# Turning queries and keys on VectorE in 32x32 blocks in place of TensorE

## What is computed

```python
xn = rms_norm(x, norm_mix[l])
proj = xn @ w_in[l]
qa, ka, va, oa, if_pre, qb, kb, vb, gates = jnp.split(proj, IN_SPLITS, axis=-1)
h_a = mlstm_chunkwise(heads(qa, 4), heads(ka, 4), heads(va, 4), ig, lf)   # 4 heads, dqk 128
qh = rms_norm(heads(qb, 8), norm_q_moba[l])                               # 8 heads, dh 128
kh = rms_norm(heads(kb, 8), norm_k_moba[l])
h_b = moba_attention(qh, kh, heads(vb, 8))
...
merged = g[..., :D] * (h_a @ w_branch_a[l]) + g[..., D:] * (h_b @ w_branch_b[l])
x = x + merged @ w_out[l]
x = x + jnp.square(jax.nn.relu(rms_norm(x, norm_mlp[l]) @ w_up[l])) @ w_down[l]
```

## Time and profile before

| | |
|---|---|
| Median of 3 runs | 1382.12 us (1382.01 to 1382.16) |
| Profiled execution | 1381.83 us, its span 1380.0 us |
| TensorE busy | 1374.2 us, 100% of the span |
| VectorE busy | 740.3 us, 54% |
| ScalarE busy | 624.2 us, 45% |
| Granted TensorE clock | full in every slice of the span |
| HBM | 187 GB/s over the span |

### The profile page before, as it was taken

The page is one execution under the profiler, slowest core; times in us unless marked ns, Lnnn a source line. Parts: engine busy times, 40 slices in busy tenths (PEclk is TensorE's granted clock), DMA queues, the critical chain, the costliest instruction groups (busy, mean ns, idle before and its releaser), DMA issues.

```text
span 1380.0 us, 17281 instructions
## 1 busy us (share of the span) xinstructions
PE 1374.2 (100%) x6655; PEld 1154.1 (84%) x6655; DVE 740.3 (54%) x741; ACT 624.2 (45%) x713; POOL 20.5 (1%) x35
## 2 busy tenths in 40 slices
PE   9999999999999999999999999999999999999999
PEld 7888888888888888888888888888888888888887
DVE  5566555544655454555565656544445656544443
ACT  5545455464444444445444444333334444443332
POOL 1111000000000000000000000000000000000000
PEclk9999999999999999999999999999999999999999
DMA  8555554545655555555555555555565555565562
GB/s 277 188 190 184 181 174 158 178 156 179 244 183 192 196 191 182 195 182 195 179 192 186 182 183 183 196 199 184 198 197 183 183 182 186 185 205 185 190 205 92
DMA packets 132549, 258.73 MB, mean 187 GB/s; under 512 B 6250, under 2 KB 8340, under 8 KB 132244
## 3 DMA queue, kind: packets, MB, share of 16 engines
q1 hardware_dynamic: 130336, 257.97, 56.5%
q10 hardware_dynamic: 2164, 0.09, 0.1%
HBM read 255.94 MB, written 2.10 MB: 187 GB/s over the span
## 4 chain that ended last, share of the span: by engine, by line
PE 99%; DMA 0%; DVE 0%; ACT 0%; issue 0%; SPq 0%; ACTq 0%
PE ps L871 23%; PE ps L873 23%; PE ps L872 23%; PE ps L894 17%; PE ps L889 9%; PE ps L903 2%; DMA rows<-in_x_dram 0%; PE ps L923 0%; PE ps L971 0%; PE ps L1028 0%; PE ps L991 0%; PE ps L990 0%; PE ps L989 0%; PE ps L970 0%; PE ps L1017 0%; PE ps L1016 0%
## 5 line engine op out<-in xcount | busy, mean ns | idle before, releaser
L603 DVE TENSOR_TENSOR w_lo<-raw,w_hi 128x1024 fp32r<-128x1024 f32 x480 | 587.6, 1225 | 601.6 <-ACT w_hi L364 600.4
L364 ACT ACTIVATE w_hi<-raw 128x1024 fp32r<-128x1024 f32 x480 | 508.9, 1061 | 722.2 <-PE ps L873 524.4
L894 PE MATMUL ps<-xT,w_hi 128*128 128x512 f32 x1024 | 360.5, 398 | 0.0
L889 PE MATMUL ps<-xT,w_lo 128*128 128x256 f32 x1024 | 284.9, 281 | 0.0
L871 PE MATMUL ps<-w_hi,xT 128*128 128x512 f32 x640 | 254.9, 398 | 0.7 <-DVE w_lo L603 0.7
L873 PE MATMUL ps<-w_hi,xT 128*128 128x512 f32 x640 | 249.7, 390 | 0.0
L872 PE MATMUL ps<-w_lo,xT 128*128 128x512 f32 x640 | 249.2, 389 | 0.0
L894 PEld LDWEIGHTS ps<-xT,w_hi 128*128 128x128 f32 x1024 | 191.4, 188 | 46.1
L889 PEld LDWEIGHTS ps<-xT,w_lo 128*128 128x128 f32 x1024 | 193.4, 189 | 1.5
L871 PE MATMUL ps<-w_hi,merged 128*128 128x512 f32 x384 | 149.7, 390 | 0.0
L871 PE MATMUL ps<-w_hi,branch 128*128 128x512 f32 x384 | 149.5, 389 | 0.0
(11 more groups left out here) (173 smaller groups left out, 586.2 us busy)
## 6 DMA issues: line engine op xcount, KB each, us to landing
raw<-in_w_in_dram SPq DMA_DIRECT2D x79, 1024.0 KB, 5.1
raw<-in_w_up_dram SPq DMA_DIRECT2D x64, 1024.0 KB, 5.4
raw<-in_w_down_dram SPq DMA_DIRECT2D x64, 1024.0 KB, 5.0
raw<-in_w_out_dram SPq DMA_DIRECT2D x16, 1024.0 KB, 5.0
raw<-in_w_branch_b_dram SPq DMA_DIRECT2D x8, 1024.0 KB, 5.0
raw<-in_w_branch_a_dram SPq DMA_DIRECT2D x8, 1024.0 KB, 5.0
rows<-in_x_dram SPq DMA_DIRECT2D x8, 256.0 KB, 7.9
rows<-in_x_dram SPq DMA_DIRECT2D x1, 2048.0 KB, 8.0
```

What stands on the lines that cost most here:

```text
L364: act.activation(w_hi[:, k % RING, :, :], raw[:, k // 2, KH * (k % 2):KH * (k % 2) + KH, :], ACT.Copy).then_inc(hi_made, 1)
L603: dve.tensor_tensor(w_lo[:, k % RING, :, :], raw[:, k // 2, KH * (k % 2):KH * (k % 2) + KH, :], w_hi[:, k % RING, :, :].bitcast(F32), ALU. ...
L889: return pe.matmul(ps[:, q0 + j, 0:S], w_lo[:, s, i, w], xT[:, t, 0, :], start=False, stop=False)
L894: last = pe.matmul(ps[:, q0 + j, :], w_hi[:, s, i, w], xT[:, t, :, :].rearrange("p a c -> p (a c)"), start=t == 0, stop=t == KT - 1)
```

## The change

TensorE no longer transposes `nat`. A new VectorE helper, `turn_quarters`, does it with 32x32 block turns: for a quarter of the source partitions (r) and a quarter of the columns of each tile (q), one instruction turns all tiles of the block, 32 partitions x 256 elements for the attention blocks (4 heads x 2 token halves x 32 columns) and 32 x 128 for the mLSTM (2 heads). A block takes 16 such instructions, eight ahead of `split_lo` at one H and eight ahead of the next. The results go to the same PSUM banks, and the copies by ScalarE stay as they were. The waits that stood in front of the transposes on TensorE now stand on VectorE.

```diff
+            def turn_quarters(dst, src, quarters, done=None):
+                dst = dst.rearrange("p (t m c) -> p m t c", m=M, c=P)
+                src = src.rearrange("p m (t c) -> p m t c", c=P)
+                for r in quarters:
+                    for q in range(0, P, 32):
+                        last = dve.transpose(dst[q:q + 32, :, :, r:r + 32], src[r:r + 32, :, :, q:q + 32])
+                if done is not None:
+                    last.then_inc(done, 1)
...
@@ jobs(H) on VectorE, for i in range(4)
+                    if H == 8 * i + 15:
+                        dve.wait_ge(nat_scaled, i + 1)
+                        if i == 1:
+                            dve.wait_ge(if_dve, 2)
+                        if i == 2:
+                            dve.wait_ge(qk_kept, 1)
+                        if i == 3:
+                            dve.wait_ge(qk_kept, 2)
+                            dve.wait_ge(if_dve, 3)
+                        turn_quarters(banks(4 + 2 * (i % 2), 6 + 2 * (i % 2)), nat[i % 2], (0, 32))
+                    if H == 8 * i + 16:
+                        turn_quarters(banks(4 + 2 * (i % 2), 6 + 2 * (i % 2)), nat[i % 2], (64, 96), qk_turned)
+                    if H == 62 + 5 * i:
+                        b = 6 + i // 2
+                        dve.wait_ge(kept[b % 2], b // 2 + 1)
+                        dve.wait_ge(qk_kept, 4 + i)
+                        if i == 0:
+                            dve.wait_ge(if_dve, 6)
+                        turn_quarters(ps[:, 7, :], nat[b % 2][:, :, S * (i % 2):S * (i % 2) + S], (0, 32))
+                    if H == 63 + 5 * i:
+                        b = 6 + i // 2
+                        turn_quarters(ps[:, 7, :], nat[b % 2][:, :, S * (i % 2):S * (i % 2) + S], (64, 96), qk_turned)
...
@@ beside(p) on TensorE, for i in range(4)
-                    if p == 8 * i + 12:
...
-                        turn_rows(4 + 2 * (i % 2), range(4), nat[i % 2], qk_turned)
-                    if p == 60 + 5 * i:
...
-                        turn_rows(7, range(2 * (i % 2), 2 * (i % 2) + 2), nat[b % 2], qk_turned)
```

More of the change, by code:

```diff
@@ L946, in beside @@
                     last.then_inc(if_pe, 1)
-                for i in range(4):
-                    if p == 8 * i + 12:
[L949 to L956, removed]
-                        turn_rows(4 + 2 * (i % 2), range(4), nat[i % 2], qk_turned)
-                    if p == 60 + 5 * i:
[L959 to L963, removed]
-                        turn_rows(7, range(2 * (i % 2), 2 * (i % 2) + 2), nat[b % 2], qk_turned)
                 for h in range(NB):
```

## The result

| | before | changed |
|---|---|---|
| Median | 1381.99 us (10 runs) | 1385.67 us (10 runs) |
| Profiled execution | 1381.83 us, span 1380.0 | 1385.25 us, span 1383.5 |

The ratio is 1.0027, 95% interval 1.0019 to 1.0036: the change costs 3.7 us, 0.27%. I had forecast 1381.5 us, no measurable change, within 1377.3 to 1391. The time lies inside the range and on the other side of the forecast.

A forecast was written before the change was run, and what follows sets the result against it. TensorE was taken as the bound, busy 1374.2 of 1380.0 us. Removed transposes, -5.24 us, plus stalls, +4.59, gave -0.65 us, from the 1382.12 median to 1381.5 us; range 1377.3 to 1391.

The forecast's parts named there:

- The removed work: TensorE, attention and mLSTM transposes: four calls of 0.87 us and four of 0.44 go, 5.24 us off, nothing hiding it.
- Nothing from the mLSTM turns: VectorE, steps 62 to 78: 16 turns per block take 3.3 us, covered by 4.8 us of idle time, no stall.
- the walk: Timeline of VectorE, ScalarE and TensorE through blocks three and four: stands of 2.56, 0.41 and 1.62 us at steps 34, 39, 40.
- the term for the stalls: TensorE waiting for VectorE's w_lo at steps 34, 39 and 40: 4.59 us in all.
- T: Time from start to start of 32x256 turns on VectorE: taken as 0.40 us, bounds 0.27 and 0.68.
- my third rival: VectorE operations don't overlap, 0.48 us per turn: stalls 7.15 us, run +1.9 us, 1384.0; inside the 0.45 of no measurable change.
- the forecast's own slope: TensorE's stalls grow by 32 us per us of turn time, between 0.30 and 0.56 us.
- wrote "nothing": Second block, steps 20 to 25: w_lo(24) meets step 24 at 86.2 up to 0.56 us per turn, so no stall.
- the forecast's line: Stalls of 4.59 us plus 32 times the turn time beyond 0.40 us, set against 5.24 us removed from TensorE.
- the middle case: Whole run: no measurable change, within 0.2% or 2.76 us, for turn times from 0.334 to 0.506 us; chance 0.45.
- Rival 2: VectorE becomes the bound around if_rows: slower, 1388.5 us at 0.60 us per turn, decides from 0.506; chance 0.35.
- Break-even: Turn time at which VectorE's added stalls equal the transposes removed from TensorE: 0.42 us.

The follow-up runs named there:

- filler series: Changed kernel plus idle TensorE matmuls behind steps 32 and 33: 9 and 20, 1385.68 us; 5 and 10, 1387.49; these plus 8 behind step 39, 1385.43.
- spread kernels: Changed kernel with turns of blocks 2 and 3 spread, two per step over eight steps: 1377.75 us; then none ahead of steps 35 and 36: 1376.58.

## Why the prediction was wrong

**Confirmed.** The removed work: 5.24 us forecast, 1.9 for the mLSTM alone (1.76), 3.7 with two blocks (3.5), 5.35 with all. Nothing from the mLSTM turns. The place: the stands come around if_rows and at the end of block 3, and the walk's order of events is the trace's: split_hi(33) waits for VectorE through the Exp, if_rows follows, step 34 stands longest. The steps are not all the forecast ones: TensorE stood ahead of 32, 33, 34 and 40, where the walk had 34, 39 and 40.

**The step that failed** is the term for the stalls, 4.59 us, where TensorE lost 7.10 standing and 1.74 at half speed, 8.84; with it the forecast of -0.65 us became +3.7. The last two runs of the filler series show that these two are one sum: it is how late VectorE's w_lo(40) is against an undisturbed TensorE. The 4.25 us missing fall to three terms:
- *T.* I took 0.40 us from eight scalar_tensor_tensor, which overlap by 0.08. A turn takes 0.47 in a burst with no overlap, as in my third rival. By the forecast's own slope, 32 x 0.067 is 2.1 us.
- *The neighbour of a burst.* The split ahead of each burst gives way after 1.23 to 1.26 us and not 1.14: four bursts, some 0.5 us. I had the price of an instruction and not what it does to the one ahead.
- *The block before.* I checked that the turns of the second block end in time for step 24, 86.2, and wrote "nothing". They do, but VectorE came to the third block some 0.7 us later against TensorE, the GpSimd operation of that block took 0.85 us more, and the scaling waited for it, 1.53 us. The wait ahead of step 32, 1.43 us, goes when block 1 goes back to TensorE. The third block's walk started at 96.86 as before, as if VectorE still stood where it did against TensorE; it should have started from where the second one left VectorE.

Together 4.0 of 4.25; the rest is not assigned. The run with turns to SBUF fits this split as an estimate: 0.02 us less per turn, 0.2 for two splits and 1.43 for the block before make 2.3 us less, and its stands come to 6.48 us, 2.36 less than 8.84.

**The chances.** With T = 0.47 the forecast's line gives +1.6 us, still the middle case; the other two terms take it over 0.2%. Rival 2, VectorE as the bound around if_rows, is what happened, but at a T of 0.47 and not from 0.506, since its threshold was worked out from a walk that gave VectorE too much lead and left out the neighbours. Break-even would have been near T = 0.36 by the same slope, with the two missing terms in. Neither I nor a rival had the granted clock in the sum. It cost nothing here, but two stands of 0.93 and 2.26 us ahead of the last step of a stretch cost 1.8 us.

**The page's price.** The estimate by the Trainium skill (VectorE: DVE Perf Modes, "The three transpose paths"), 0.43 us, was nearer than mine; the trace shows 0.456 in the mean and 0.323 for 128 columns, against 311 ns for a bf16 turn. The section "The DRAIN you can't avoid" of the same page says that the next operation doesn't start until the pipe is empty, and adds that one which isn't held starts earlier. I took it without the second half and set it aside for the row of eight, which doesn't contradict the whole. In the bursts each turn follows the end of the last, 0.47 us apart at 0.456 each; behind turns read from partition 0 the spread kernels show the earlier start.

## What to carry over

When work is moved to an engine that feeds the bound one, add up its queue over several rounds from one common start, and carry the lead that one round has used into the next; "done in time" is not "without effect". The amount of the moved work mattered less than its place: the same 128 instructions cost 3.7 us with the 32 of blocks 2 and 3 in bursts of eight around a serial chain, and gain 5.35 us with these 32 in twos and threes away from it. And the price of an unknown instruction is better bounded without overlap, with a little taken from its neighbour, than from a row of another operation that overlaps with itself: the eight of that row all cover the same 128 partitions, and the turns don't.

## What the runs showed of the hardware

- A float32 block turn on VectorE takes 0.456 us in the mean for 32x256 and 0.323 us for 32x128; 128 more columns take 0.13 us, so by that slope some 0.19 us are the instruction's own.
- The same pieces as copies start 0.43 us apart to PSUM and 0.30 us apart within SBUF. I had not expected the target to matter that much.
- A VectorE operation can start some 0.1 us before the last has ended: behind splits of 1.23 us after 1.13 or 1.14, behind turns of 0.45 to 0.46 us that read from partition 0 after 0.37. Within a burst none does, nor behind turns that read from another quarter of the partitions.
- A GpSimd operation on 128x8 takes 2.5 us where two splits run back to back on VectorE beside it, and 1.64 us where they don't.
- TensorE's granted clock fell to the 1.2 GHz level for 3.4 us each time after it had stood 1.4, 1.3 and 2.6 us ahead of three steps in a row, after 1.3 and 2.6 us in the run without block 1, after 0.97 and 2.58 us in the run with copies to PSUM, and after 0.93 and 2.26 us in two steps; it stayed full when idle matmuls filled such stands, and after single stands of 1.1 and 1.8 us. In the profiled execution with turns to SBUF two stands of 1.16 and 2.58 us by step 34 brought no fall, and two of 0.66 and 2.07 us by step 40 did; what decides between such cases stays open.
